# Masked attention and index of the second block: dropping the corner no query sees, pairing heads, and keeping the index's weights stationary

## The reference, cut to what matters

```python
def masked_softmax(s, mask):
    s = jnp.where(mask, s.astype(jnp.float32), -jnp.inf)
    return jax.nn.softmax(s, axis=-1)

# branch A, 8 heads of 64; start = 0 or 128 (blocks of 128 queries)
s_own = einsum('bhqd,bhkd->bhqk', qb, k_own) * scale
m_own = kpos_own[None, :] <= qpos[:, None]
o = einsum('bhqk,bhkd->bhqd', masked_softmax(s_own, m_own), v_own)

# branch B, 8 heads of 64; index of 8 heads of 64, n_sel = 64
rel = jax.nn.relu(einsum('bqhd,bsd->bqhs', qi_b, ki))
idx_score = einsum('bqhs,bqh->bqs', rel, wi_b)
idx_score = where(kpos[None, :] <= qpos[:, None], idx_score, -inf)
_, sel = lax.top_k(idx_score, n_sel)
valid = sel <= qpos[None, :, None]
p = masked_softmax(einsum('bqhd,bqnhd->bqhn', q_b, kg) * scale, valid)

wi = i_w * (IDX_HEADS ** -0.5)      # i_w = h @ w_in[:, 8 columns]
```

## Time and profile before

| | us |
|---|---|
| median of three executions | 2848.55 (2846.83 to 2848.88) |
| the profiled execution | 2847.8 |
| its span in the trace | 2846.0 |
| PE busy | 2687.8 (94%) |
| DVE, ACT, POOL busy | 1682.9, 1226.7, 676.6 |
| mean granted clock of TensorE | 0.964 |

### The profile page before, as it was taken

How to read it: one execution, slowest core, us unless ns; L and a number is a source line. 1 busy time by engine, 2 the same in 40 slices (tenths; PEclk the granted TensorE clock), 3 DMA queues, 4 the chain that set the end, 5 groups by cost and what they waited for, 6 DMA issues and landing times.

```text
span 2846.0 us, 43440 instructions
## 1 busy us (share of the span) xinstructions
PE 2687.8 (94%) x16880; PEld 2305.4 (81%) x16880; DVE 1682.9 (59%) x2966; ACT 1226.7 (43%) x2333; POOL 676.6 (24%) x614
## 2 busy tenths in 40 slices
PE   8999999988789999999999998999989999899998
PEld 5778887867777888887887876899988988798877
DVE  5775557878665774447543455565544656546666
ACT  4223225631254333225333235655445575544773
POOL 1111121012134111112111221121244424645224
PEclk9999999998779999999999998999989999999999
DMA  6553531210012453433434422345534433434334
GB/s 253 170 181 133 174 130 54 88 38 2 1 60 89 156 172 116 166 102 129 157 130 147 156 87 69 112 156 180 177 97 136 148 109 127 149 111 148 108 109 133
DMA packets 115869, 352.85 MB, mean 124 GB/s; under 512 B 12753, under 2 KB 14929, under 8 KB 115281
## 3 DMA queue, kind: packets, MB, share of 16 engines
q1 hardware_dynamic: 115664, 350.08, 36.7%
HBM read 348.98 MB, written 1.05 MB: 123 GB/s over the span
## 4 chain that ended last, share of the span: by engine, by line
PE 71%; DVE 10%; ACT 7%; issue 6%; POOL 3%; DMA 3%; SPq 1%; DVEq 0%; ACTq 0%; POOLq 0%
PE ps L1755 19%; PE ps L1758 18%; PE ps L1756 18%; ACT spl L2083 2%; DMA ring<-w_stream 2%; DVE spl L2326 2%; PE ps L1820 1%; PE ps L1797 1%; DVE big L2543 1%; POOL bigr L2797 1%; PE ps L1835 1%; POOL spl L2792 1%; PE ps L1829 1%; PE ps L2037 1%; ACT big L2267 1%
## 5 line engine op out<-in xcount | busy, mean ns | idle before, releaser
L1755 PE MATMUL ps<-bigr,spl 128*128 128x256 f32 (+1 forms) x3880 | 1331.7, 343 | 41.0 <-DVE spl L2326 15.1
L1758 PE MATMUL ps<-bigr,spl 128*128 128x256 f32 (+1 forms) x3880 | 1309.1, 337 | 6.8 <-POOL bigr L2797 6.5
L1756 PE MATMUL ps<-bigr,spl 128*128 128x256 f32 (+1 forms) x3880 | 1306.0, 337 | 0.0
L2326 DVE TENSOR_TENSOR spl<-ring,spl 128x512 fp32r<-128x512 f32 x840 | 677.7, 814 | 684.0 <-ACT spl L2083 681.1
L2083 ACT ACTIVATE spl<-ring 128x512 fp32r<-128x512 f32 x1024 | 625.3, 625 | 764.1 <-PE ps L1758 555.8
L1755 PEld LDWEIGHTS ps<-bigr,spl 128*128 128x128 f32 x3880 | 744.9, 192 | 148.1 <-issue 39.3
L1758 PEld LDWEIGHTS ps<-bigr,spl 128*128 128x128 f32 x3880 | 744.9, 192 | 89.3 <-POOL bigr L2797 14.4
L1756 PEld LDWEIGHTS ps<-bigr,spl 128*128 128x128 f32 x3880 | 745.9, 192 | 73.9 <-issue 1.5
L2797 POOL TENSOR_TENSOR bigr<-work,bigr 128x512 fp32r<-128x512 f32 (+1 forms) x208 | 218.8, 1055 | 996.0 <-ACT bigr L2087 995.9
L2792 POOL TENSOR_TENSOR spl<-ring,spl 128x512 fp32r<-128x512 f32 x184 | 252.7, 1375 | 354.0 <-ACT spl L2083 353.8
L2087 ACT ACTIVATE bigr<-work 128x512 fp32r<-128x512 f32 (+2 forms) x240 | 123.7, 517 | 316.9 <-DVE work L2411 168.0
(11 more groups left out here) (303 smaller groups left out, 2520.8 us busy)
## 6 DMA issues: line engine op xcount, KB each, us to landing
ring<-w_stream SPq DMA_DIRECT2D x512, 512.0 KB, 3.4
big<-w_stream SPq DMA_DIRECT2D x256, 256.0 KB, 3.3
big<-w_stream SPq DMA_DIRECT2D x16, 512.0 KB, 11.4
X<-x_t SPq DMA_DIRECT2D x2, 1024.0 KB, 14.0
cst<-consts SPq DMA_DIRECT2D x1, 1601.5 KB, 6.9
X<-mem_t SPq DMA_DIRECT2D x1, 1024.0 KB, 5.8
out_t<-X SPq DMA_DIRECT2D x8, 128.0 KB, 2.1
prm<-params SPq DMA_DIRECT2D x1, 252.5 KB, 2.8
```

The lines of the kernel that those rows point to most:

```text
L1755: pe.matmul(out, hi, x[0], start=k == 0, stop=False)
L1756: pe.matmul(out, lo, x[0], start=False, stop=False)
L1758: finish(pe.matmul(out, hi, x[1], start=False, stop=k == nk - 1), tile, key if k == nk - 1 else None)
L2326: dve.tensor_tensor(lo_half(h), raw_half(h), hi_half(h), SUB).then_inc(*sig("lo", h, by="lo_dve"))
```

## The change

1. The masks (`causal`, the index's sum, the selection) have 128 + 256 columns instead of 256 + 256; scores, exponentials, ReLU, maxima and normalization of masked heads and of the index work on these 384.
2. Transposes of a masked head are three instead of four; its values are three products of 128 query columns instead of two of 256.
3. Masked heads and index heads are taken two at a time: the four score products alternate between the even head (array rows 0 to 63) and the odd one (64 to 127), each with a bank of its own. A slot with two heads is followed by one with none. The normalization on DVE is ordered so that both heads are masked and reduced before the first exponential is waited for. There is a fourth buffer for probabilities.
4. The index's weights are the stationary operand (8 columns), the activations stream 256 columns; the result (8 x 256) is copied out by ACT and turned back by two small products, after the next projection.

Memory attention and the first block's attention go through the same functions with their old sizes, one head a time.

```diff
-    q = np.concatenate([p[:, None] + 128 * n >= np.arange(L)[None, :] for n in range(2)], 1)
+    q = np.concatenate([p[:, None] + 128 * n >= np.arange(128 * n + 128)[None, :] for n in range(2)], 1)
...
-                a, c = [], []
-                for it in list(items) + [None, None, None]:
+                a, c, slots, lag = [], [], [], 1
+                for it in items:
+                    slots += [it, ()] if len(it) > 1 else [it]
+                    lag = len(it)
+                n = 0
+                while a or c or n < len(slots):
                     if c:
                         yield from values(*c.pop(0))
-                    if len(a) > 1 or a and it is None:
+                    if len(a) > lag or a and n >= len(slots):
                         i0, sc = a.pop(0)
                         c.append((i0, (yield from turn(i0, sc))))
-                    if it is not None:
-                        a.append((it, (yield from scores(it))))
+                    if n < len(slots) and slots[n]:
+                        yield from scores(slots[n])
+                    n += 1
                     yield CUT
...
-                WKI, IDX, SEL = (B(5120 + 512 * i, 512) for i in range(3))
-                PB = Rot(tiles_at(6656, 3, 512))
+                WKI, IDX, SEL = (B(5120 + 512 * i, 384) for i in range(3))
+                PB = Rot(tiles_at(6656, 3, 512) + [B(29952, 512)])
...
-                    yield "index_weights", l, b, free, tile, src, fl
-                    banks.give(bi, ("wi", l))
+                    yield "index_weights", l, b, free, tile, src
+                    wt, wfree, wti = tmps.get()
+                    yield "evacuate", ("index_weights", l), wt[0:8, 0:L], b[0:8, 0:L], [("wi_mm", l)] + wfree
...
+                    later.append(index_turn)
...
-                for i, q in enumerate(it["q"]):
-                    ins = pe.matmul(b[:, i * nk:(i + 1) * nk], q, it["k"], start=True, stop=True)
-                ins.then_inc(*sig("scores", u))
+                spans = entries[0][1]["spans"]
+                for i, (s0, s1) in enumerate(spans):
+                    for u, it, b, *_ in entries:
+                        ins = pe.matmul(b[:, s0:s1], it["q"][i], it["k"][:, 0:s1 - s0], start=True, stop=True)
+                        if i == len(spans) - 1:
+                            ins.then_inc(*sig("scores", u))
...
+                    v = it["v"]
+                    pe.matmul(o[:, 0:128], v[0], pt[:, 0:128], start=True, stop=True)
+                    pe.matmul(o[:, 128:256], v[0], pt[:, 128:256], start=True, stop=False)
+                    ins = pe.matmul(o[:, 128:256], v[1], pt[:, 256:384], start=False, stop=True)
...
-                for i in range(2):
-                    for k in range(KD):
...
-                        pe.matmul(out, xh, hi[:, 8 * k:8 * k + 8], start=k == 0, stop=False)
-                        pe.matmul(out, xh, lo[:, 8 * k:8 * k + 8], start=False, stop=False)
-                        ins = pe.matmul(out, xl, hi[:, 8 * k:8 * k + 8], start=False, stop=k == KD - 1)
+                out = b[0:8, 0:L]
+                for k, (xh, xl, need) in enumerate(src):
+                    w.all(need, done)
+                    wh, wl = hi[:, 8 * k:8 * k + 8], lo[:, 8 * k:8 * k + 8]
+                    pe.matmul(out, wh, xh, start=k == 0, stop=False)
+                    pe.matmul(out, wl, xh, start=False, stop=False)
+                    ins = pe.matmul(out, wh, xl, start=False, stop=k == KD - 1)
+                finish(ins, tile, ("wi_mm", l))
+
+            def index_turn(l, wt, b, free, fl):
+                w.wait_ge(*done("evac", "index_weights", l))
+                w.all(free, done)
                 for i in range(2):
+                    ins = pe.matmul(b[:, 8 * i:8 * i + 8], wt[0:8, 128 * i:128 * i + 128], P("ident")[0:8, 0:8], start=True, stop=True)
+                ins.then_inc(*sig("wi_t", l))
...
-            def index_head(l, h, q, k, b, need, rl, rfree, IDX):
+            def index_heads(l, heads, need, IDX):
                 w.all(need, done)
-                for i in range(2):
-                    ins = pe.matmul(b[:, 256 * i:256 * i + 256], q[i], k, start=True, stop=True)
-                ins.then_inc(*sig("idx_mm", l, h))
+                for h, q, k, (b, free, bi), _ in heads:
+                    w.all(free, done)
+                for i, (s0, s1) in enumerate(((0, 128), (128, 384))):
+                    for h, q, k, (b, free, bi), _ in heads:
+                        ins = pe.matmul(b[:, s0:s1], q[i], k[:, 0:s1 - s0], start=True, stop=True)
```

More of the change, by code:

```diff
@@ L1191, in attend, with scores @@
             def attend(items, PB, PT):
-                def scores(it):
-                    nq = len(it["q"])
-                    b, free, bi = banks.get()
-                    p, pfree, pi = PB.get()
-                    st, sfree, si = stats.get()
-                    u = new()
-                    yield "scores", u, it, b, free, p, pfree, st, sfree
-                    banks.give(bi, ("masked", u) if it["mask"] else ("exp", u))
-                    stats.give(si, ("p", u))
-                    return u, p, pi
+                def scores(its):
+                    entries, res = [], []
+                    for it in its:
+                        b, free, bi = banks.get()
+                        p, pfree, pi = PB.get()
+                        st, sfree, si = stats.get()
+                        u = new()
+                        entries.append((u, it, b, free, p, pfree, st, sfree))
+                        res.append((it, (u, p, pi), bi, si))
+                    yield "scores", entries
+                    for it, (u, p, pi), bi, si in res:
+                        banks.give(bi, ("masked", u) if it["mask"] else ("exp", u))
+                        stats.give(si, ("p", u))
+                        a.append((it, (u, p, pi)))
                 def turn(it, sc):
@@ L2035, in values @@
                 w.all(it["vneed"], done)
-                for k, v in enumerate(it["v"]):
-                    ins = pe.matmul(o, v, pt[:, k * n:(k + 1) * n], start=k == 0, stop=k == len(it["v"]) - 1)
+                if not it["mask"]:
+                    n = len(it["q"]) * 128
+                    for k, v in enumerate(it["v"]):
+                        ins = pe.matmul(o, v, pt[:, k * n:(k + 1) * n], start=k == 0, stop=k == len(it["v"]) - 1)
+                else:
+                    v = it["v"]
+                    pe.matmul(o[:, 0:128], v[0], pt[:, 0:128], start=True, stop=True)
+                    pe.matmul(o[:, 128:256], v[0], pt[:, 128:256], start=True, stop=False)
+                    ins = pe.matmul(o[:, 128:256], v[1], pt[:, 256:384], start=False, stop=True)
                 ins.then_inc(*sig("av", u))
@@ L2273, in probs_turn @@
                 w.all(ptfree, done)
-                act.activation(pt, b, ACTF.Copy).then_inc(*sig("ptc", u))
+                n = sum(s1 - s0 for s0, s1 in it["spans"])
+                act.activation(pt[:, 0:n], b[:, 0:n], ACTF.Copy).then_inc(*sig("ptc", u))
             def gated(l, piece, m, dst, b, fn, need):
@@ L2279, in gated, with index_heads @@
                 act.activation(dst, b, fn).then_inc(*sig("gated", l, piece, m))
-            def index_head(l, h, q, k, b, need, rl, rfree, IDX):
-                w.wait_ge(*done("idx_mm", l, h))
-                w.all(rfree, done)
-                act.activation(rl, b, ACTF.Relu).then_inc(*sig("relu", l, h))
+            def index_heads(l, heads, need, IDX):
+                for h, q, k, (b, free, bi), (rl, rfree, ri) in heads:
+                    w.wait_ge(*done("idx_mm", l, h))
+                    w.all(rfree, done)
+                    act.activation(rl[:, 0:384], b[:, 0:384], ACTF.Relu).then_inc(*sig("relu", l, h))
             run({f.__name__: f for f in (
@@ new lines, in scores @@
+            def scores(entries):
+                for u, it, b, free, p, pfree, st, sfree in entries:
+                    src, n, spans = b, len(it["q"]), it["spans"]
+                    w.wait_ge(*done("scores", u))
+                    w.all(sfree, done)
+                    if it["mask"]:
+                        mask, need = it["mask"]
+                        w.all(pfree, done)
+                        w.all(need, done)
+                        dve.tensor_tensor(p[:, 0:384], b[:, 0:384], mask, ADD).then_inc(*sig("masked", u))
+                        w.wait_ge(*done("masked", u))
+                        src = p
+                        dve.tensor_reduce(st[:, 0:1], src[:, 0:128], AXX, ALU.max)
+                        link(dve.tensor_reduce(st[:, 1:2], src[:, 128:384], AXX, ALU.max))
+                    else:
+                        link(dve.tensor_reduce(st[:, 0:n], src.rearrange("p (i k) -> p i k", i=n), AXX, ALU.max))
+                    linked()
+                    dve.tensor_scalar(st[:, 2:2 + n], st[:, 0:n], -it["scale"], None, MUL).then_inc(*sig("nmax", u))
```

(8 more changed lines are left out.)

149 lines of the change are left out of this document (68 added, 81 removed).

## The result

| | before | after |
|---|---|---|
| median, us | 2847.69 (2846.75 to 2848.88) | 2800.75 (2797.68 to 2805.49) |
| executions | 4 | 4 |
| ratio, 95% interval | | 0.9836 (0.9819 to 0.9853) |
| profiled execution, us | 2847.8 | 2799.46 |

The changed kernel is 46.9 us faster; 2793 was forecast, with 2779 to 2818 as the range. The page of the profile after answers to the earlier trace rows. They start at its first product, the one that waits 6.8 us for GpSimd (POOL) in every trace. In the fourteen traces of this document this product starts anywhere from 2073.6 to 2084.2 us, though the first block does the same work in all, so a cut at one fixed time would mix the first block's variation into the second block's time.

A forecast was written before the change was run, and what follows sets the result against it. PE's own instructions were taken to bound the second block; 20.2 + 10.1 + 2 + 3.5 + 6.7 + 15.4 - 1.4 + 4 - 5 = 55.5 us saved gave 2793 against the median, range 2779 to 2818.

The forecast's parts named there:

- Scores and index heads: Masked and index head pairs overlap fully in two row halves, 0.84 us a pair: 20.2 and 10.1 us saved.
- rival 1: Score products of the two row halves stream one after the other; 24 pairs save 15.4 us less, 2808; chance 0.15.
- Values and transposes: Masked heads: one transpose fewer each saves 3.5 us, values as three products of 128 columns save 6.7.
- The index's weights: Index weights and the projection behind them, both layers: 30.2 us become 14.8, saving 15.4; the turn back costs 1.4.
- Rival 3: The index's weights stay at the low clock or cost more than a projection's pieces; about 2800 us; chance 0.08.
- change of shape: Every second slot of a branch loses its score and array shape changes: 24 x 0.09 = 2 us saved.
- I count back 4 of the 8.4: PE's waits for ACT's gate activations, 8.4 us before: 4 us saved, as exponentials would stand behind the gates.
- I charge 5 us of new waits: Slots become shorter than the weight copies' reserve: 5 us of new PE waits for weights.
- rival 5: Late pair exponentials delay ACT's gates; PE waits at a bank every pair, 4.9 us each: 2875; chance 0.03.
- DVE stands 9.5 us in eight heads for that, hidden mostly: Before the change, DVE waits 9.5 us in eight heads for exponentials, mostly hidden; masking both heads first avoids this.
- Rival 2: DVE becomes the bound of the masked slots at 5.8 us a head; 18 us come back, 2811; chance 0.12.
- Rival 4: All PE waits shrink together, no new ones come, the clock falls less often: 12 us below forecast, 2781; chance 0.06.

The follow-up runs named there:

- e11: Changed kernel with masked heads paired 0 with 2, 4 with 6, 1 with 3, 5 with 7, both in the same array rows; 2801.39 us.
- e3: Changed kernel without pairs: one masked head or index head a slot; 2814.57 us, 0.9891 of the kernel before.
- e6: Changed kernel with DVE's old order: mask, maxima, wait for the exponential and normalize one head, then the next; 2837.90 us.
- e7: Changed kernel with the second head's exponential and normalization a slot later and an empty slot ahead of a branch's first pair; 2785.47 us.
- e9: e7 with both heads' transposes in the slot without scores and their values by turns in the next; 2778.67 us.
- e1: Changed kernel with the empty slot put ahead of each masked pair's scores instead of behind; 2801.05 us, 0.9844 of the kernel before.

## Why the prediction was right, and where it was not

- **Scores and index heads, 30.3 us.** Right in mechanism and size: 0.856 a pair for 0.84. e11 makes the 16 masked pairs what rival 1 described, 1.50 a pair for my 1.48. The 10 us that rival 1 asks for them are 9.7 on PE, but only 3.5 in the block. The 0.2 a pair that I set beside the sum for weight loads did not appear.
- **Values and transposes, 10.2 us.** Values 0.80 as forecast. Four transposes between values and a score take 0.586 before, three 0.477 in e3: 0.11 a head, as forecast.
- **The index's weights, 15.4 us.** 13.5 us for my 14.8, and the turn 0.54 a layer for 0.7: 15.6 net for 14.0. I had the clock down ahead of the products in both layers; that held in layer one (4.54 us for my 4.4) and not in layer two (3.00). Rival 3 is out: with the 8 columns as the stationary side the products come at 0.12 us, as a projection's do, and the clock comes back on the way.
- **PE in sum.** The terms on PE came to 56.5, and its busy time fell by 58.6. (The "some 50" among my signs did not follow from that sum.) Besides the index's weights, the change of shape was sized too small. Transposes take 0.477 ahead of a score and 0.303 ahead of a projection, so each masked slot that lost its score saves 0.17 where I had 0.09.
- **The waits, "I count back 4 of the 8.4" and "I charge 5 us of new waits".** This is the step that failed: in place of +1 there were +12.2. Halves took 9.1 more instead of 5 and, at 18.5, passed the 15 us I had set as a bound; gates gave back nothing and took 1.7 more, 10.1 where I had set 5. Copies ahead of values, for which the sum had no term, took 2.8. I took the new order of exponentials and gates from places where the pair's scores stand behind the gates. In four pairs they stand between the two projections of a gate pair, and there rival 5's mechanism did occur, at 2.3 to 2.5 us a pair; it stayed far below the 3.7 us in every pair from which it decides.
- **"DVE stands 9.5 us in eight heads for that, hidden mostly".** Hidden before, as far as PE's waits of 9.4 for halves and 8.4 for gates tell. With pairs the same order costs 37 us (e6). The new order in DVE was the condition for most of the gain, and my sum had no term for it.
- **Rival 2** put its 18 us on DVE's own work. DVE was busy 58% of the block; it was the round trip from DVE to ACT and back that counted, in ACT's queue.
- **Rival 4** (2781) did not occur. e7 comes near it (2785) by moving steps alone, and e9 reaches it (2779) with the values by two besides.

The total came within 8 us of the forecast, and in part by an offset: PE's work fell by 2.1 more than my terms, which hid some of the missing 11 us of the waits.

What stays open: how much of e9's 51 us of idle time is ACT's load and how much its order, and why the first block takes up to 10 us more in one trace than in another. A larger reserve of weight halves would tell the first; a fifth half needs 4 KB more a partition, and no run tried it.

## What to carry to other kernels

When work is taken off the bounding engine, price the longest in-order block on the engines that feed it, at the new slot length: here the pairs took 23 us off PE and brought 14 by medians (12 in the traced block). Moving one exponential a slot later, with the pairs on the right side of the gates, brought 15 more by medians (10 in the block). An instruction that waits for another engine costs what is queued behind it, so put a slot between the one's result and the other's use. Ask of every overlap whether the resource below is still the bound; e11 put 9.7 us of PE's work back, and 3.5 of it showed. And cut a stretch at the same instruction in every trace, not at the same time: a cut at 2080 us makes e1 look 5.5 us shorter than after, where its block is 0.7 us shorter.

## What was not expected of the hardware

- Products in different row halves overlap in any order of issue, up to a whole head of four pieces apart (0.862 us head by head, 0.856 by turns, 1.504 in the same rows).
- Column halves with different moving data overlap as well: 0.806 us for two heads' values, 0.800 for one.
- Products with 8 stationary and 256 moving columns (fp32r) take 0.125 us each, 3.00 for 24, and load in less time than they stream (0.09 us in the record, 0.12 from start to start); the same work with 8 moving columns took 9.2 to 10.5 us for 48.
